# Reordering the first layer of a two-layer fp32 decoder trunk: low parts, a late rounding, an activation table load and two row broadcasts change places

## The reference

```
proj = x @ w_in                      # 1024 x 6160: xm, z, o_pre (2048 each), gates i, f
xc   = silu(causal_dwconv(xm))       # 4 taps along the tokens
q, k = xc_head @ w_q, xc_head @ w_k  # 8 heads of 256 channels; q and k are 128 wide
v    = xm_head @ w_v                 # 256 wide
h    = mlstm_chunkwise(q, k, v, i, f)   # 8 chunks of 128 tokens, one after the other
hb   = sigmoid(o_pre) * normalise(h) * g + skip * xc
out  = (hb * silu(z)) @ w_out
```

## Time and profile before

| | |
|---|---|
| median of 3 runs | 1390.37 us (1390.35 to 1393.38) |
| profiled execution, its own time | 1389.8 us |
| its span, first to last instruction | 1388.0 us |
| TensorE busy | 1365.6 us (98%) |
| VectorE busy | 1116.6 us (80%) |
| ScalarE busy | 834.5 us (60%) |
| granted TensorE clock, mean | 0.999 |

### The profile page before, as it was taken

The page is one execution under the profiler, slowest core; times in us unless marked ns, Lnnn a source line. Parts: engine busy times, 40 slices in busy tenths (PEclk is TensorE's granted clock), DMA queues, the critical chain, the costliest instruction groups (busy, mean ns, idle before and its releaser), DMA issues.

```text
span 1388.0 us, 18976 instructions
## 1 busy us (share of the span) xinstructions
PE 1365.6 (98%) x6490; PEld 1138.1 (82%) x6490; DVE 1116.6 (80%) x1841; ACT 834.5 (60%) x1390; POOL 145.9 (11%) x246
## 2 busy tenths in 40 slices
PE   9999999999999999999999999999999999999997
PEld 7888788888888887788888888888888888888886
DVE  7878888897988888788774456797888888899976
ACT  5877778787886878779743436564333333446340
POOL 1001011010101111010000001001111111100021
PEclk9999999999999999999999999999999999999999
DMA  6117355272634627356497666334566555699661
GB/s 235 49 39 171 96 124 144 76 178 89 166 100 92 174 69 166 107 149 193 135 327 246 224 195 217 128 123 128 146 173 163 148 146 153 176 289 340 211 203 76
DMA packets 133377, 220.77 MB, mean 159 GB/s; under 512 B 40578, under 2 KB 57474, under 8 KB 132130
## 3 DMA queue, kind: packets, MB, share of 16 engines
q1 hardware_dynamic: 120482, 186.01, 42.3%
q0 software_dynamic: 12800, 33.56, 12.7%
HBM read 170.11 MB, written 75.63 MB: 177 GB/s over the span
## 4 chain that ended last, share of the span: by engine, by line
PE 83%; DVE 9%; DMA 3%; ACT 3%; issue 2%; POOL 0%; SPq 0%; DVEq 0%; ACTq 0%; POOLq 0%
PE wide L2951 17%; PE wide L2953 17%; PE wide L2952 17%; DMA in_raw<-in_w_in 3%; PE ps_state L2951 3%; PE ps_state L2953 3%; PE ps_state L2952 3%; PE ps_inter L2951 2%; PE ps_inter L2952 2%; PE ps_inter L2953 2%; PE ps_intra L3130 2%; PE ps_intra L2953 2%; PE ps_s L2953 2%; PE ps_s L2951 2%; PE ps_intra L2951 2%
## 5 line engine op out<-in xcount | busy, mean ns | idle before, releaser
L2952 PE MATMUL wide<-xa,inb 128*128 128x512 f32 x576 | 224.6, 390 | 0.0
L2951 PE MATMUL wide<-xb,inb 128*128 128x512 f32 x472 | 189.4, 401 | 2.2 <-ACT z_buf L1238 1.3
L2953 PE MATMUL wide<-xb,inb 128*128 128x512 f32 x472 | 184.2, 390 | 0.0
L2952 PEld LDWEIGHTS wide<-xa,inb 128*128 128x128 f32 x576 | 108.4, 188 | 20.4
L2952 PE MATMUL wide<-xa,blk 128*128 128x512 f32 x320 | 124.5, 389 | 0.0
L2951 PEld LDWEIGHTS wide<-xb,inb 128*128 128x128 f32 x472 | 88.8, 188 | 22.2 <-DVE inb L1985 3.7
L2953 PEld LDWEIGHTS wide<-xb,inb 128*128 128x128 f32 x472 | 88.6, 188 | 19.0
L2951 PE MATMUL wide<-xb,blk 128*128 128x512 f32 x256 | 99.6, 389 | 0.0
L2953 PE MATMUL wide<-xb,blk 128*128 128x512 f32 x256 | 99.6, 389 | 0.0
L1904 ACT ACTIVATE wy<-wy_raw 128x1024 fp32r<-128x1024 f32 x56 | 59.4, 1062 | 61.1 <-DMA wy_raw<-y_block 60.7
L2951 PE MATMUL wide<-xa,inb 128*128 128x512 f32 x208 | 83.5, 401 | 0.7 <-DVE inb L1985 0.7
(11 more groups left out here) (435 smaller groups left out, 3931.1 us busy)
## 6 DMA issues: line engine op xcount, KB each, us to landing
in_raw<-in_w_in SPq DMA_DIRECT2D x45, 512.0 KB, 4.2
wy_raw<-y_block SPq DMA_DIRECT2D x56, 256.0 KB, 4.4
mw_raw<-h_block SPq DMA_DIRECT2D x53, 256.0 KB, 3.3
m_sum<-in_w_out POOLq DMA_DIRECT2D x48, 256.0 KB, 4.3
h_block<-f_buf SPq DMA_DIRECT2D x48, 256.0 KB, 3.7
w_sum<-in_pool_w_out POOLq DMA_DIRECT2D x48, 256.0 KB, 4.2
a_raw<-in_pool_w_z SPq DMA_DIRECT2D x16, 512.0 KB, 4.1
a_raw<-folded SPq DMA_DIRECT2D x16, 512.0 KB, 4.4
```

What stands on the lines that cost most here:

```text
L2951: pe.matmul(dst, a[0], b[0], start=first, stop=False, skip_group_check=more)
L2952: pe.matmul(dst, a[0], b[1], start=False, stop=False, skip_group_check=more)
L2953: return pe.matmul(dst, a[1], b[0], start=False, stop=last, skip_group_check=more)
```

## The change

Five things are reordered; nothing is computed otherwise.

1. SP: `load_rows(h)` is issued behind `move_turned(h-1, 1)` and `load_in(3h+2, 1)`, not ahead of them.
2. ACT, `second_half`: `high_qkv(h)` goes ahead of the four-fold `join_turn` steps. DVE: `low_qkv(h)` goes ahead of `y_turned(h-1, 0)`.
3. ACT, `second_half`: the snapshot of quadrant 6 goes ahead of `high_xc(h, 1)`. Behind `silu_z(h, 3)` come `silu_conv(h, 0)`, `high_xc(h, 0)`, the Exp table load, both `skip_term`, and only then `in_high(x + 21)`.
4. DVE, `second_half`: `in_low(x + 20)` goes ahead of `h_difference(h-1, 7)`; the differences 6 and 4 go behind the taps and `low_xm(h, 0)`.
5. ACT, head 0: `high_xm` is woven around `silu_conv(0, 0)`, and `in_high(13)`, `silu_z(0, 3)` and the table load go behind the skip terms.

```diff
--- before.py
+++ after.py
@@ -865,9 +865,9 @@
                 move_turned(h - 1, 0)
                 load_qkv(h)
                 load_in(3 * h + 2, 0)
-                load_rows(h)
                 move_turned(h - 1, 1)
                 load_in(3 * h + 2, 1)
+                load_rows(h)
                 store_h(h - 1, 1, 2, 5, 3, 7)
                 if h < HEADS - 1:
                     load_in(3 * h + 3, 0)
@@ -1483,10 +1483,10 @@
                 x = AT_A[3 * h + 2, 1] - 14
                 in_high(x + 15)
                 in_snapshot(3 * h + 1, 6)
+                high_qkv(h)
                 join_turn(h - 1, 0, 0)
                 join_turn(h - 1, 0, 1)
                 in_upper_right(3 * h)
-                high_qkv(h)
                 in_snapshot(3 * h + 1, 5)
                 in_high(x + 16)
                 join_turn(h - 1, 1, 0)
@@ -1504,15 +1504,15 @@
                 high_xm(h, 0)
                 in_upper_right(3 * h + 1)
                 high_xm(h, 1)
+                in_snapshot(3 * h + 2, 6)
                 high_xc(h, 1)
-                in_snapshot(3 * h + 2, 6)
                 silu_z(h, 3)
+                silu_conv(h, 0)
+                high_xc(h, 0)
+                act.preload_act_table(ACT.Exp)
+                skip_term(h, 1)
+                skip_term(h, 0)
                 in_high(x + 21)
-                silu_conv(h, 0)
-                skip_term(h, 1)
-                high_xc(h, 0)
-                skip_term(h, 0)
-                act.preload_act_table(ACT.Exp)
 
             def next_head(h):
 
@@ -1666,17 +1666,17 @@
             silu_z(0, 1)
             silu_z(0, 2)
             in_snapshot(2, 6)
+            high_xm(0, 0)
             silu_conv(0, 0)
+            high_xm(0, 1)
             in_copy(1, 0, 1)
-            high_xm(0, 0)
-            in_high(13)
-            high_xm(0, 1)
-            silu_z(0, 3)
-            act.preload_act_table(ACT.Exp)
             skip_term(0, 1)
             high_xc(0, 1)
             high_xc(0, 0)
             skip_term(0, 0)
+            in_high(13)
+            silu_z(0, 3)
+            act.preload_act_table(ACT.Exp)
             in_high(14)
             decay(0, 0)
             in_snapshot(2, 5)
@@ -2291,6 +2291,7 @@
 
                 x = AT_A[3 * h + 2, 1] - 14
                 tap(h, 1, 3)
+                low_qkv(h)
                 y_turned(h - 1, 0)
                 y_finish(h - 1, 0)
                 y_turned(h - 1, 1)
@@ -2301,7 +2302,6 @@
                 in_low(x + 16)
                 in_low(x + 17)
                 in_sum(3 * h + 2, 2)
-                low_qkv(h)
                 in_sum(3 * h + 2, 3)
                 y_turned(h - 1, 2)
                 in_low(x + 18)
@@ -2312,13 +2312,13 @@
                 h_difference(h - 1, 5)
                 y_finish(h - 1, 3)
                 tap(h, 0, 1)
+                in_low(x + 20)
                 h_difference(h - 1, 7)
-                h_difference(h - 1, 6)
-                in_low(x + 20)
-                h_difference(h - 1, 4)
                 tap(h, 0, 2)
                 tap(h, 0, 3)
                 low_xm(h, 0)
+                h_difference(h - 1, 6)
+                h_difference(h - 1, 4)
                 low_xm(h, 1)
                 in_join(3 * h + 2, 2)
                 low_xc(h, 1)
```

## The result

| | before | after |
|---|---|---|
| median | 1390.37 us | 1403.41 us (1399.12 to 1405.83, 5 runs) |
| profiled execution, its span | 1388.0 us | 1401.6 us |
| TensorE busy | 1365.6 us | 1371.1 us |
| granted clock, mean | 0.999 | 0.993 |

The ratio of after to before is 1.0091, with a 95% interval of 1.0077 to 1.0105. It compares fast runs alone: of the five runs of the kernel before beside it one took 4777.46 us and is not among them. The forecast was 1387.4 us; the measured time is 16 us above it and 8 above the range.

What follows compares the result with a forecast made beforehand. TensorE, busy 98% of the span, bounds the kernel; its waits allow at most 14.9 us. Terms -6.0 + 4.1 - 2.8 + 2.0 - 0.3 = -3.0 us took the median from 1390.4 to 1387.4 us, range 1379.5 to 1395.5.

Steps and rivals of the forecast that it cites:

- Part 1: Ahead of the values: differences 6 and 4 behind low_xm(h, 0) remove the wait in heads 1 to 6, -6.0 us.
- Part 2: Ahead of the queries: the later store of quadrant 4 holds the skip terms; with the mask's delay, +4.1 us.
- w: The queries' wait for the store of quadrant 4 in a head: L - 1.5 = 1.4 us with the mask.
- L: The time the store of quadrant 4 takes, taken as 2.9 us, between 2.0 and 6.2.
- Part 3: Rows broadcast later: snapshot waits go, -2.8 us; GpSimd's mask costs DVE 0.8 us, 0.4 of it delaying difference 4.
- Rival C: Late rows delay the weights in front of them, DVE 1.3 us late in six heads: +7.8, 1395.2 us; chance 0.07.
- Part 4: high_qkv ahead of the joins delays in_upper_right(3h) by 0.95 us: zero, or up to 0.3 us a head without cover.
- Part 5: Head 7: the 1 MB load goes out later, so the keys start later, +2.0 us net.
- Part 6: Head 0: the wait ahead of the queries goes, but low_v(0, 1) limits the keys, -0.3 us.
- Rival A: The store of quadrant 4 holds skip_term and decides: at 5.1 us it gives 1400.6 us, slower; chance 0.13.

Runs made afterwards that it cites:

- rows_back: The changed kernel with load_rows issued where it was before the change, ahead of the second transpose; 1389.75 us, ratio 1.0002.
- fill_wait: The changed kernel with 20 idle transposes on TensorE ahead of the queries, in heads 1 to 7; 1398.18 us, ratio 1.0067.
- qkv_alone: The kernel before with only the roundings of q, k and v moved (high_qkv ahead of the joins, low_qkv ahead of y_turned); 1387.66 us, ratio 0.9979.
- six_ahead: The changed kernel with rows in their old place and difference 6 ahead of low_xm(h, 0), difference 4 behind it; 1385.92 us, ratio 0.9974.
- sums_held: The changed kernel with GpSimd's weight sums stopped ahead of the values in heads 1 to 6, not in head 7; 1392.67 us, ratio 1.0013.

## Why the prediction was wrong

**Part 1 was right.** No wait of PE stands ahead of the values; seven waits (5.9 + 1.1 us) went, head 7's too.

**Part 2 is the step that failed, in size and not in mechanism.** It named the store of quadrant 4 as the next thing late, and every one of the seven waits goes back to it. It put w at 1.4 us; the idle alone was 2.4 (median of seven), and w, counted as the forecast counted it, 2.5. Two terms were small. The store was due 0.46 us behind the values' start and went out 0.9 behind it, 1.2 in head 3. Part 1 had credited 0.7 us for the earlier `low_qkv`; but `high_qkv` ahead of the joins makes the join late (DVE's step behind it starts 19.8 us ahead of the values instead of 20.8), and 0.5 us were left: that is what `rows_back` shows, where the sum starts at 300.04 and the values at 313.11. The mask took 0.9 us and not 0.4. The two make 0.7, head 3's difference. And L was 3.5 us, not 2.9: I had taken the middle because "one of those two neighbours is gone". The weights nearly were (0.7 us of overlap at most); but the sums, which part 3 itself delays, took their place. With the rows back the same formula holds (0.4 behind the start, L = 3.0, and 1.36 us of idle, all by the median). The rest of the chain was well sized: 3.8 us from landing to queries was forecast, and from 318.8 + 5.2 = 324.0 to 327.86 in head 3 is 3.9.

**A term was missing: the clock.** I costed a wait at its idle and 0.16 us. Waits of 2.25 to 4.3 us were followed by half clock in four heads of seven, and that added 6.0 us. `fill_wait` gave back 3.3 to 5.2.

**Part 3 was right on the snapshots** (2.2 us gone) **and on the price of one mask** (0.9 us against 0.8), wrong on its cover. I let 0.4 us fall on DVE's idle ahead of the sum; in five heads of seven the mask now meets a low part (303.12 in head 3), in the other two a sum of weights. Behind it, in head 3, DVE has no idle at all up to the values. The Trainium skill (SBUF - State Buffer, "Who interferes with whom") has a VectorE instruction with two SBUF inputs contend with a GpSimd instruction that reads SBUF, and the order of issue decide who is blocked; the low part started 0.3 us into the mask of 1.35 us and lost 0.9, which agrees. Rival C didn't show: no instruction of DVE waits for weights. What the step lacked altogether is who stands behind the mask on GpSimd's queue.

**Part 4** is zero in six heads; in head 1 TensorE waited 0.9 us for `in_upper_right`, three times the 0.3 that I allowed without cover. ACT had stood 1.75 us for the weights of product x+14 there (2.38 before), and in `qkv_alone`, where it stood 0.19, TensorE doesn't wait there: the late weights have a part in it. **Part 5** had the size right by luck and the place wrong. The net delay of head 7, apart from the clock, was 1.9 us against 2.0: -1.0 ahead of the values, +2.4 at the queries, which wait for the store like the others, and only +0.5 at the keys. **Part 6** was right, head 0's wait is gone, and its keys start 0.6 us earlier (0.3 forecast).

**By the corrected sizes:** w of heads 1 to 6 adds to 16.9 us against 8.4 (+8.5), the clock +6.0, the low parts beside the mask +0.9, L1253 +1.1, and what else differs adds to about nothing. That is 16.5 us. The profiled execution was to take 1386.8 us; 1403.3 comes out, and it took 1403.4.

**Rival A was the one.** It gave 1400.6 for L = 5.1 at a chance of 0.13, and set the point for a measurable loss at L = 4.1. Its reasoning was right ("a GpSimd transfer is in flight in every head"); its threshold inherited the early store and had no clock in it, so that 3.5 sufficed. Its time lay 5 us above the end of my range.

## What to carry to other kernels

When a step is moved back, its consumer's slack has to cover the step *and* the transfer behind it, at the length that transfer has among its new neighbours; list who else is moved to that moment, above all what stands behind a waiting instruction on another engine's queue. Price a wait of some us on TensorE with the clock that follows it, and put harmless matmuls there if the wait must stay. And measure a bundle of reorderings in pieces: here three of five parts gave 0.55%, and the other two hid it.

## What the runs showed of the hardware

- Behind a wait the clock fell for stretches of 3.4 us (once 6.8). Idle alone doesn't tell when: in the changed kernel 2.25 and 2.71 us were followed by a fall, 2.31 and 2.38 us were not; in `six_ahead` 2.06 us was, in `sums_held` 2.06 us was not; in `fill_wait` 1.92 us behind the transposes was. A stretch of 3.4 us cost 1.6 us where TensorE worked through it.
- In head 3 a 256 KB store took 2.0 us beside the store issued 0.7 us ahead of it (`sums_held`), and 5.2 us where a 256 KB accumulating transfer of GpSimd was in flight as well (the changed kernel). In head 7, with 1 MB loaded behind it, such a store took 3.3 us with no GpSimd transfer in flight (`rows_back`) and 5.1 with one (`sums_held`).
- A GpSimd instruction of 1.35 us made a DVE subtraction beside it 1.58 us long instead of 0.69 (head 3 of the changed kernel).
